# Side products in full 128x128 shape, a mask written by VectorE, and gemm tiles taken two at a time in the latent attention

## What is computed

```python
def token_mix(h, pos, lw, rel_bias, cache):
    qa, ka, va, ub, cq, ckv, kpe, ud, gate_in = split_cols(h @ lw['w_in'])
    q = (rmsnorm(cq, lw['c_q_norm']) @ lw['w_uq']).reshape(B, T, C_HEADS, C_NOPE_DIM + C_ROPE_DIM)
    q_pe = rope(q[..., C_NOPE_DIM:], pos)
    ...
    # o_a: swa_prompt or swa_sample: 8 heads of 64, 2 key heads, 64-token chunks, a window of 2 chunks
    # o_c: mla_prompt or mla_attend: 8 heads over one latent, a key is visible if its chunk <= the query's
    ...
    merged = (gates[:, :, 0] * (o_a @ lw['w_o_a']) + gates[:, :, 1] * (o_b @ lw['w_o_b'])
              + gates[:, :, 2] * (o_c @ lw['w_o_c']) + gates[:, :, 3] * (o_d @ lw['w_o_d']))
    return merged @ lw['w_out']
for l in range(2):
    x = x + token_mix(rmsnorm(x), ...)
    x = x + swiglu(rmsnorm(x), w_ff_gate[l], w_ff_up[l], w_ff_down[l])
```

## Time and profile before

| | |
|---|---|
| time before, median of 3 runs | 2490.18 us (2490.05 to 2490.38) |
| the profiled execution | 2506.54 us, its span 2504.7 us |
| PE busy | 2376.0 us (95%), 15160 matmuls |
| PEld busy | 2220.4 us (89%) |
| DVE / ACT / POOL busy | 1291.9 (52%) / 860.1 (34%) / 953.3 us (38%) |
| chain that ended last | PE 89%, DVE 6%, issue 2%, ACT 1% |
| mean granted TensorE clock | 0.97 |

### The profile page before, as it was taken

How to read it: one execution, slowest core, us unless ns; L and a number is a source line. 1 busy time by engine, 2 the same in 40 slices (tenths; PEclk the granted TensorE clock), 3 DMA queues, 4 the chain that set the end, 5 groups by cost and what they waited for, 6 DMA issues and landing times.

```text
span 2504.7 us, 40008 instructions
## 1 busy us (share of the span) xinstructions
PE 2376.0 (95%) x15160; PEld 2220.4 (89%) x15160; DVE 1291.9 (52%) x2296; ACT 860.1 (34%) x1688; POOL 953.3 (38%) x988
## 2 busy tenths in 40 slices
PE   6997999999999899999979989999999999999996
PEld 5996998777899899999979969987779999999996
DVE  6976243333225953826479752433332378366374
ACT  2014233334212553625410142333333145345252
POOL 3551454222166233332445415532224642423231
PEclk9999999999699999999989989999999999999998
DMA  5341121011023122222234311211012322222121
GB/s 173 113 129 52 55 73 55 26 39 39 19 97 121 51 93 70 84 92 68 69 114 139 107 32 64 68 51 38 27 38 64 113 76 75 86 76 93 61 88 55
DMA packets 70131, 186.78 MB, mean 75 GB/s; under 512 B 19648, under 2 KB 22304, under 8 KB 68960
## 3 DMA queue, kind: packets, MB, share of 16 engines
q1 hardware_dynamic: 53280, 162.23, 20.1%
q10 hardware_dynamic: 16704, 22.52, 2.7%
HBM read 172.41 MB, written 14.14 MB: 74 GB/s over the span
## 4 chain that ended last, share of the span: by engine, by line
PE 89%; DVE 6%; issue 2%; ACT 1%; ACTq 0%; DMA 0%; SPq 0%; DVEq 0%
PE gemm L641 44%; PE gemm L1057 16%; PE gemm L1047 13%; PE side L1057 3%; PE side L909 2%; PE side L930 2%; PE side L860 1%; DVE rstd L1613 1%; PE side L910 1%; PE side L790 1%; DVE act_lo L2038 1%; PE side L869 1%; PE side L917 1%; DVE prod L1642 1%; PE side L711 1%
## 5 line engine op out<-in xcount | busy, mean ns | idle before, releaser
L604 POOL CAST w_hi<-w_raw 128x384 fp32r<-128x384 f32 x376 | 213.0, 566 | 895.8 <-PE gemm L641 874.6
L621 POOL TENSOR_TENSOR ring_lo<-w_raw,ring_hi 128x512 fp32r<-128x512 f32 x232 | 307.9, 1330 | 590.3 <-ACT ring_hi L1475 590.3
L606 POOL TENSOR_TENSOR w_lo<-w_raw,w_hi 128x384 fp32r<-128x384 f32 x376 | 435.7, 1159 | 30.1
L641 PE MATMUL gemm<-h_hi,w_hi 128*128 128x320 f32 x1728 | 423.1, 326 | 20.1 <-DVE h_lo L1619 16.8
L641 PE MATMUL gemm<-h_lo,w_hi 128*128 128x320 f32 x1728 | 398.5, 312 | 0.0
L641 PE MATMUL gemm<-h_hi,w_lo 128*128 128x320 f32 x1728 | 398.1, 312 | 0.0
L641 PEld LDWEIGHTS gemm<-h_hi,w_hi 128*128 128x128 f32 x1728 | 290.4, 191 | 49.7 <-issue 36.3
L1057 PE MATMUL gemm<-act_hi,ring_hi 128*128 128x320 f32 x960 | 299.4, 312 | 19.0 <-issue 9.9
L1057 PE MATMUL gemm<-act_lo,ring_hi 128*128 128x320 f32 x960 | 298.7, 311 | 0.0
L1057 PE MATMUL gemm<-act_hi,ring_lo 128*128 128x320 f32 x960 | 298.4, 311 | 0.0
L641 PEld LDWEIGHTS gemm<-h_lo,w_hi 128*128 128x128 f32 x1728 | 294.1, 191 | 0.0
(11 more groups left out here) (280 smaller groups left out, 4247.0 us busy)
## 6 DMA issues: line engine op xcount, KB each, us to landing
w_raw<-in_ws_ff SPq DMA_DIRECT2D x120, 512.0 KB, 3.2
w_raw<-in_ws_gate SPq DMA_DIRECT2D x64, 512.0 KB, 3.3
w_raw<-in_ws_in SPq DMA_DIRECT2D x44, 512.0 KB, 3.3
w_raw<-in_ws_proj SPq DMA_DIRECT2D x64, 256.0 KB, 2.6
w_raw<-in_ws_out SPq DMA_DIRECT2D x16, 512.0 KB, 3.3
w_raw<-in_ws_fd SPq DMA_DIRECT2D x16, 384.0 KB, 3.0
x_park<-x ACTq DMA_DIRECT2D x2, 2560.0 KB, 12.1
x<-x_park ACTq DMA_DIRECT2D x4, 1280.0 KB, 5.8
```

Of the source, the lines that this page charges most:

```text
L604: eng.tensor_copy(w_hi[s][:, cols], w_raw[s][:, cols]).then_inc(w_high.sem, 1)
L606: eng.tensor_tensor(w_lo[s][:, cols], w_raw[s][:, cols], w_hi[s][:, cols].bitcast(F32), ALU.subtract).then_inc(w_split.sem, 1)
L621: eng.tensor_tensor(lo, src, hi.bitcast(F32), ALU.subtract).then_inc(lo_plain.sem, 1)
L641: mm = eng.matmul(dst[:, hf, 0:HALF], w, r[:, k, cols], start=first and k == 0 and part == 0, stop=last and k == kk - 1 and part == 2)
```

## The change

It does six things. (1) Products of 64 rows or 64 columns get the full 128x128 shape by zeros or by a second, unused half: `a_scores` for the prompt (keys padded with zeros in a second plane of `k_window`), `keys` for h > 0, `values` (two heads' columns, of which one is read), `sample_queries`, the rope part of the sample scores, the samples' second transpose and second value product. (2) The mask matmul is gone: VectorE writes -2^100 into the 64x64 corner of the scores in PSUM before it takes the maximum, and waits for that write. (3) `spread` for heads 1 to 7 becomes 2, 0, 1, 2, 0, 1, 2, 0, 1, 0, 2, 1, so that `queries` and a turn, `keys` and a turn, `sample_queries` and a turn follow each other. (4) `new_rows` takes its four transposes first and its four half-shape matmuls after. (5) Smaller: the keys of the window are copied by four ScalarE instructions of 64 rows and stored by two DMAs; the query copy L1916 and one copy per sample go; three memsets zero the padding before the convolution. (6) Some buffers move, and w_uk and the rope cache are loaded with their zero rows (512 KB for 256 KB each).

```diff
-        kT, o = sb("k_window", [P, NP], F32, o)
+        kT, o = sb("k_window", [P, 2, NP], F32, o)
...
-                eng.dma_start(wuk[64:128, :, :], one("w_uk")).then_inc(wts_loaded.sem, 16)
+                eng.dma_start(wuk[:, :, :], one("w_uk")).then_inc(wts_loaded.sem, 16)
...
+                    if j < 8:
+                        out = bank[:, 0:4 * w].rearrange("p (v c k) -> p v c k", v=2, c=2)
+                        for c in range(2):
+                            mm = eng.matmul(out[:, :, c, :], qT[:, 256 * j + P * c:256 * j + P * c + P],
+                                            kT[:, :, 64 * (j + 1) - w:64 * (j + 1)], start=True, stop=True)
...
-                    eng.matmul(bank[64:128, :], wukt[:, 64 * h:64 * h + 64], ckvT[:, 0:NP], start=True, stop=True)\
+                    rows, first = (bank[64:128, :], 0) if h == 0 else (bank[:, :], 64 * h - 64)
+                    eng.matmul(rows, wukt[:, first:64 * h + 64], ckvT[:, 0:NP], start=True, stop=True)\
...
-                    eng.matmul(bank[:, 0:NS], wuk[64:128, h, :], qns[64:128, :], start=True, stop=True)\
+                    eng.matmul(heads(bank[:, 0:NS]), wuk[:, h, :], qps[:, :, h, :], start=True, stop=True)\
...
-                    spread = iter((1, 0, 1, 1, 0, 1, 1, 0, 1, 0, 1, 1) if h == 0 else (1,) * 12)
+                    spread = iter((1, 0, 1, 1, 0, 1, 1, 0, 1, 0, 1, 1) if h == 0 else (2, 0, 1, 2, 0, 1, 2, 0, 1, 0, 2, 1))
...
-                        eng.matmul(bank[:, 0:w], qh[h % 2][:, P * i:w], kh[h % 2][:, 0:w], start=True, stop=False)
-                        eng.matmul(bank[:, w - CHUNK:w], mask_q[:, :], mask_k[:, :], start=False, stop=True)\
+                        eng.matmul(bank[:, 0:w], qh[h % 2][:, P * i:w], kh[h % 2][:, 0:w], start=True, stop=True)\
...
-                            mm = eng.matmul(B[6][part, i * P:(i + 1) * P], v_tok[k][:, 64 * h:64 * h + 64],
+                            mm = eng.matmul(B[6][:, i * P:(i + 1) * P], v_tok[k][:, two],
                                             PT[i % 2][:, k * P:(k + 1) * P], start=(k == 0), stop=(k == i))
...
-                    eng.matmul(bank[:, PAST:PAST + NQ], qp, kpeT[0:64, new], start=False, stop=True)\
+                    eng.matmul(bank[:, PAST:PAST + NQ], qp, kpeT[:, new], start=False, stop=True)\
...
-                    eng.transpose(bank[0:NQ, P:2 * P], S[b % 2][:, PAST:PAST + NQ], ident[:, :]).then_inc(side.sem, 1)
+                    eng.transpose(bank[:, P:2 * P], S[b % 2][:, P:2 * P], ident[:, :]).then_inc(side.sem, 1)
...
-                    eng.activation(PT[b % 2][:, 0:P], bank[:, 0:P], ACT.Copy)
-                    eng.activation(PT[b % 2][0:NQ, P:2 * P], bank[0:NQ, P:2 * P], ACT.Copy).then_inc(freed(("St", b)), 1)
+                    eng.activation(PT[b % 2][:, 0:2 * P], bank[:, 0:2 * P], ACT.Copy).then_inc(freed(("St", b)), 1)
...
+                eng.memset(ntk[:, :, :], 0.0).then_inc(pads.sem, 1)
+                eng.memset(kT[64:128, 0, :], 0.0).then_inc(pads.sem, 1)
+                eng.memset(kT[0:64, 1, :], 0.0).then_inc(pads.sem, 1)
...
                 def c_front(n, name, w):
                     bank = filled(eng, l, name)
+                    if n < 4 * NH:
+                        eng.memset(bank[0:CHUNK, w - CHUNK:w], -BIG).then_inc(c_step.sem, 1)
+                        eng.wait_ge(c_step.sem, c_step.at(l, c_order[("m", n)]))
```

More of the change, by code:

```diff
@@ L474, in layer_of, with heads @@
             return ap[bass.ds(i, 1)].rearrange(f"z y {dims} -> (z y) {dims}")
+        def heads(ap):
+            return ap.rearrange("p (h q) -> p h q", q=NQ)
         def whole(t):
@@ L753, in new_rows @@
                     bank = fill(l, ("new", half))
+                    tokens = [slice(NP + NQ * b, NP + NQ * b + NQ) for b in range(4 * half, 4 * half + 4)]
                     for n in range(4):
-                        tokens = slice(NP + NQ * (4 * half + n), NP + NQ * (4 * half + n) + NQ)
-                        eng.transpose(bank[0:NQ, n * P:(n + 1) * P], ckvT[:, tokens], ident[:, :])
-                        mm = eng.matmul(bank[64:SKEYS, n * P:(n + 1) * P], vT[:, tokens], ident[:, :],
+                        eng.transpose(bank[0:NQ, n * P:(n + 1) * P], ckvT[:, tokens[n]], ident[:, :])
+                    for n in range(4):
+                        mm = eng.matmul(bank[64:SKEYS, n * P:(n + 1) * P], vT[:, tokens[n]], ident[:, :],
                                         start=True, stop=True)
@@ L778, in a_scores @@
                         eng.sem_inc(passed["pe"], 1)
[L779 to L794, removed]
+                    if j < 8:
[3 more added lines that the diff above has]
+                                            kT[:, :, 64 * (j + 1) - w:64 * (j + 1)], start=True, stop=True)
+                    else:
+                        for c in range(4):
+                            b = 4 * (j - 8) + c
+                            for kv in range(2):
+                                part = slice(64 * kv, 64 * kv + 64)
                                 mm = eng.matmul(bank[part, c * w:(c + 1) * w],
@@ L918, in turn @@
                         mm.then_inc(side.sem, 1)
-                    part = slice(64 * (h % 2), 64 * (h % 2) + 64)
+                    two = slice(P * (h // 2), P * (h // 2) + P)
                     def values(i):
@@ L987, in s_values @@
                     eng.matmul(bank[:, 0:P], cct[:, b, :], PT[b % 2][:, 0:P], start=True, stop=False)
-                    eng.matmul(bank[:, 0:P], ntk[:, b, :], PT[b % 2][0:NQ, P:2 * P], start=False, stop=True)\
+                    eng.matmul(bank[:, 0:P], ntk[:, b, :], PT[b % 2][:, P:2 * P], start=False, stop=True)\
                        .then_inc(side.sem, 1)
@@ L1252, in _ @@
                 read_unit(eng, l, 17)
-                eng.dma_start(out("o_k_p"), kT[:, NP - P:NP]).then_inc(kv_out.sem, 16)
+                for kv, part in enumerate((slice(0, 64), slice(64, 128))):
+                    eng.dma_start(out("o_k_p")[part, :], kT[part, kv, NP - P:NP]).then_inc(kv_out.sem, 16)
                 eng.dma_start(out("o_v_p"), vT[:, NP - P:NP]).then_inc(kv_out.sem, 16)
@@ L2262, in lay_out @@
         "ident": np.eye(P, dtype=np.float32), "ones": np.ones((P, P), np.float32),
-        "dup": np.tile(np.eye(32, dtype=np.float32), (2, 4)),
+        "dup": cat([np.tile(np.eye(32, dtype=np.float32), (2, 2)), np.zeros((64, 64), np.float32)], 1),
         "cs": rotary(), "hot": buckets(),
```

57 lines of the change are left out of this document (25 added, 32 removed).

## The result

The changed kernel takes 2426.72 us, the median of four runs (2423.99 to 2428.05), against 2490.28 of the kernel before beside it: the ratio is 0.9721, with a 95% interval from 0.9686 to 0.9756. 68 us were forecast and 63.6 came. The profiled execution took 2427.87 us, its span 2426.1. Of the 39 executions of the kernel before that were timed in this study, 22 took 2490 to 2494 us, 11 some 17 us and 6 some 35 us longer, about one or two times the 17.96 us that half rate in one layer's samples cost in the earlier trace rows; none of the other kernels shows such steps.

The account below looks back on a forecast made before the run. PE's own stream was taken to bound the kernel. Savings of 21.4 (heads), 6.8 (window) and 6.0 (samples) less 0.15 gave 34.0 us a layer, 68 in all: 2490.2 to 2422 us, range 2414 to 2430, reaching 2408 and 2440.

Parts of the forecast that it names:

- What a head's stream costs: One head on PE: 10240 side columns at 0.84 ns, 8.60 us, plus twelve tiles, 10.58 us: 19.18 us.
- What the change removes: Heads: PE draining between shapes should go, 4.36 us of the measured 23.54 us a head.
- The wait on the values of block 2: Every head: PE waits 1.4 us for ScalarE's copy of turn 2, behind keys copy, table load and sigmoid.
- Turn 0's wait: Start of a head: PE waits 0.2 us for VectorE's scaling behind two new memsets, 0.5 by the upper price.
- Samples: Sample stage: 3.55 us a sample becomes 2.77, 0.78 saved six times, plus 1.3 at start and end: 6.0 a layer.
- Window attention: Window scores: 0.8 us saved six times, about as much on chunks 0 and 1; with `new_rows`, 6.8 a layer.
- 1.2 for `new_rows`: `new_rows` loses six of eight shape changes a layer, some 0.2 us each: 1.2 us saved.
- ScalarE's first pool copy: The fifth key DMA delays this copy by at most half a us; 0.15 us a layer taken as loss.
- the rivals on the clock: Clock halves in samples of one or both layers: 2436 or 2450, chance 0.13; in the heads: up to 2720, 0.04.
- The waits came: Heads, rival that the waits don't come and PE's stream alone bounds: 28 us less, 2394, chance 0.05.
- no longer than two a head: Heads, rival of more waits than two a head: 0.6 us more a head, 2432, chance 0.10.
- Loads that show: Heads, rival that doubled weight loads cost 0.025 us each: 8 us, 2430 (2439 by the skill's rate), chance 0.03.

Follow-up runs that it names:

- the merge later: Changed kernel with single tiles, turn 2's copy ahead of the sigmoid, and VectorE's merge moved behind the next head's block 0 scaling: 2397.63 us, heads 149.18.
- The kernel before with pairs: Kernel before with only the tile order changed, two at a time in heads 1 to 7: 2502.59 us, heads 187.04.
- the two profiled variants of before: Kernel before with only tiles two at a time (2502.59 us), and kernel before with only the mask product replaced by VectorE's memset (2463.86 us).

## Why the prediction was right, and where it was off

**What a head's stream costs: right.** The basis, 0.84 ns a column and 0.88 us a tile with nothing between full-shape pieces, gave 19.18 us. With the merge later, which leaves neither wait in heads 1 to 6, a head takes 19.27 us. The 0.09 over is the error of that term.

**What the change removes: right in sum, and now by part.** In the heads of one layer: the mask product 13.8 us (measured alone, with turn 0's new wait taken off), the values' half shape 8.9 (measured alone, in the order with pairs), and by difference, 167.92 - 8.91 - 153.42, 5.6 for keys and sample queries. Together 28.3 us a layer; where the line between the last two lies is open by some tenths of a us a head, as the values were measured beside a wait. Window, `new_rows` and samples are read from the traces, and no run takes them out alone. The 0.92 us of overhead that rows 3 gave for one stretch was the right signal.

**The wait on the values of block 2: right in place, cause and number, undersized in price.** Forecast 1.4, recorded 1.28 and worth 1.54. Turn 0's wait was worth 0.36 for 0.2. These and the stream's 0.09 are 0.4 us a head: 21.17 instead of 20.8, and with heads 0 and 7 most of the 3.2 us a layer by which the heads missed. The wait was priced as idle time, where its cost is read from the start of the piece ahead of it to the start of the gemm behind it.

**Where the wait comes from.** The prediction took it as the price of thinner tiles, which it is. What it did not ask is what the pairs give in return. The experiments' answer is nothing: 10.1 us a layer lost in the changed kernel, 5.3 in the kernel before, and no gain when the wait is taken away by other means (152.46 and 152.39 us). The whole change is a gain of some 28 us a layer in the heads with a loss of 10 laid over it.

**Samples: the term was mis-sized.** 4.5 us a layer for 6.0. Three steps of a sample came out longer by 0.06, 0.06 and 0.08 us. The first is the one copy for two, which ends 0.85 us after the turn's start instead of 0.80, with the scores 0.06 behind it. The second is the scores' own length: they were taken at the pace of their loads with no margin. The third is the way from scores to the next turn, which I had left as it was. Over the six samples from the first turn to the seventh that makes 3.4 us saved for 4.7 forecast (0.78 each); start and end gave 1.1 for 1.3.

**Window attention: right, once the clock is taken out.** From the first window scores to head 0 the kernel before takes 190.38 us, the changed one 181.83. The kernel before with pairs, whose window stage is unchanged, shows why that is more than the 5.6 forecast for the stage (first before, then before with pairs, both in layer 1; the granted clock is the third number from the end):

```profile
248.07:438.45 190.38, 187.05 (x1253) 173.94 (x1253) 71.59 (x148) 57.99 (x107) 89.66 (x114) 0.98 0.19 60
```

```profile
252.89:440.11 187.22, 183.91 (x1253) 171.27 (x1253) 70.07 (x148) 58.01 (x107) 90.56 (x114) 1.00 0.20 61
```

With the same instructions at a granted clock of 1.00 the stage takes 187.22 us: 5.4 to the changed kernel. The other 3.2 us are clock: the first scores of before, from 248.07 to 251.42, and the gemms behind them up to 255.3, ran at granted clocks of 0.59 and 0.50 (half rate, 1.2 GHz), after a wait of 1.37 us; those of the changed kernel, after the same wait, at 1.00. Layer 2 of before has the long form too (190.14 us), and so has layer 2 of the kernel with pairs (190.49); neither layer of the changed kernel has it. The prediction had put no clock there.

**The sum.** 18.2 for the heads, 4.5 for the samples, 5.4 for the window and 1.2 for `new_rows` (2.1 us to 1.5 in each half, as forecast) are 29.3 us a layer, 58.6 in all. For ScalarE's first pool copy nothing goes off: in layer 1 it comes 5.92 us after the first gemms' end instead of 5.45, but PE's fourth pool product starts 17.6 us after the first side product behind those gemms in both kernels (185.12 to 202.72, and 185.67 to 203.26), and in layer 2 the copy isn't late. Timed were 63.6. The clock in the first scores, up to 6.4, and the clock between the first gemms and the window scores, which start anywhere from 247.2 to 252.9 us in the profiled executions, lie between the two; which share each has in the timed runs stays open. The forecast of 68 was 9 too high in its steps, and that it came within 5 of the time is in part luck, helped by the clock.

**The rivals.** The clock held in the samples (0.99 and 1.00), and in the heads at 1.00 in spite of PE's waits, so neither of the rivals on the clock came. Nor did it halve in the samples of the two profiled variants of before. The waits came, and were no longer than two a head. Loads that show would make the stream longer than its columns by 0.5 us a head; it was longer by 0.09. The padding was free: the memsets of 0.91, 0.48 and 0.48 us stand ahead of a convolution that still finds VectorE idle for 4.08 us.

## What to carry to other kernels

Where TensorE sets the time, count its stream in columns and look for stretches that are longer than their columns. Here a product in a smaller shape cost 0.3 us or more beyond its columns, and a wider product with zeros or unused outputs was the cheaper one. Then ask of every reordering what each piece between two dependent steps was covering: the tiles taken away from between keys and values cost 10 us a layer of the 28 that the rest of the change gave in the heads. And look at the order on the engine that is waited for: two calls swapped on ScalarE, where a copy stood behind a table load that nobody was in a hurry for, gave back 23 us, as much as undoing the order of PE's tiles. Last, price a product or a wait by what its removal gives, start to start, and ask what else the removal has moved: the 0.43 us of the mask product was 0.55 less a wait that came with the memset.

## What was not expected of the hardware

- A recorded wait of 1.28 us on PE was worth 1.54 us of its stream.
- A 64-column float32 product in full shape, added between scores and a gemm, took 0.22 us from start to start, twice the 0.107 of its two instructions' columns.
- Going into 64 output columns cost about 0.1 us and coming out of them 0.2; the one-row product cost 0.55 to 0.58 us for its 64 columns, though its own record says 0.43.
- Four more changes between side products and gemms a head, all in full shape, cost nothing that shows (152.39 against 152.46 us over eight heads). A gemm's first pair has 0.38 instead of 0.29 us to the next one there, but it starts as much too early: in head 4 of the changed kernel, from turn 1 at 522.54 to the second pair at 523.05 are 0.51 us, the 256 columns of the turn (0.215) and a pair (0.294).
- The table load took 1.28 us and the sigmoid started 0.01 us after it, with the copy of the keys ending 0.02 ahead. The Trainium skill ("ScalarE: Activation LUTs", What ACT_TABLE_LOAD costs) adds a drain of about 1.4 us to each switch; no such gap stands in these rows.
